# Hybrid diffusion backbone, layer 2: the norm of tile 3 in front of the last scan unit's sums, and the table of further items behind the first item's rows

## The reference, cut to what matters

```python
y = y_f + flip(y_b) + xh * p['ssd_d'][:, None]
return rmsnorm(y * jax.nn.silu(z), p['ssd_norm_w'])            # SSD heads
...
h = head_layernorm(h_f + flip(h_b), p['ml_norm_w'])            # mLSTM heads
out = jax.nn.sigmoid(o) * h
...
xl = xl + mod_l[2] * (yl @ w_out[i])
xl = xl + mod_l[5] * hier_moe(modulated_norm(xl, norm2_w[i], mod_l[3], mod_l[4]), p)
```

## Time and profile before

| | |
|---|---|
| median of 3 runs | 1429.89 us (1426.48 to 1433.22) |
| profiled execution | 1429.08 us |
| its span, first to last instruction | 1427.2 us |
| TensorE matmuls busy | 1200.9 us (84%) |
| VectorE busy | 636.2 us (45%) |
| ScalarE busy | 301.0 us (21%) |
| mean granted clock of TensorE | 0.913 of full speed |

### The profile page before, as it was taken

One profiled execution on the slowest core, in us unless ns is written; L12 is line 12 of the kernel. 1 busy time (PEld: TensorE's weight loads), 2 busy tenths in 40 slices (PEclk: granted clock), 3 DMA queues, 4 the chain that ended last, 5 costly groups with the idle time before them and its releaser, 6 DMA issues. The chain is left out here.

```text
span 1427.2 us, 19787 instructions
## 1 busy us (share of the span) xinstructions
PE 1200.9 (84%) x7656; PEld 789.3 (55%) x7656; DVE 636.2 (45%) x1253; ACT 301.0 (21%) x614; POOL 128.3 (9%) x144
## 2 busy tenths in 40 slices
PE   3899999999899679898877579998869599788882
PEld 1444547987678554544444266467658355445551
DVE  3424763127873542343322264844383634333333
ACT  3302012254442201131101132122432100000001
POOL 0000000000000012212212100000000112222210
PEclk8899999998989769999999879999989589999996
DMA  8743132145641538999999745343472668999993
GB/s 291 199 130 118 59 104 89 57 144 184 199 149 36 226 117 332 398 358 385 383 375 378 285 163 166 118 132 104 154 235 103 227 246 318 397 381 386 394 386 126
DMA packets 148149, 322.18 MB, mean 226 GB/s; under 512 B 28443, under 2 KB 111448, under 8 KB 123864
## 3 DMA queue, kind: packets, MB, share of 16 engines
q1 hardware_dynamic: 136568, 304.86, 59.0%
q0 software_dynamic: 11392, 15.77, 3.4%
q10 hardware_dynamic: 96, 0.26, 0.0%
HBM read 321.11 MB, written 21.23 MB: 240 GB/s over the span
## 5 line engine op out<-in xcount | busy, mean ns | idle before, releaser
L635 PE MATMUL bank<-hT,ring 128*128 128x512 f32 (+1 forms) x544 | 205.9, 536 | 1.5 <-issue 0.8
L635 PE MATMUL bank<-ring,qkT 128*64 128x256 f32 x976 | 156.4, 410 | 33.3 <-DMA ring<-in_moe_w_up 18.5
L635 PE MATMUL bank<-ring,hT 128*128 128x256 f32 (+1 forms) x928 | 180.2, 349 | 3.9 <-DVE ysum L1718 2.1
L635 PEld LDWEIGHTS bank<-ring,hT 128*128 128x128 f32 x928 | 154.0, 193 | 22.6 <-ACT hT L1347 2.7
L635 PEld LDWEIGHTS bank<-hT,ring 128*128 128x128 f32 x544 | 104.1, 193 | 97.9 <-issue 91.1
L1718 DVE TENSOR_TENSOR xbc<-xbc,bank 64x256 f32<-64x256 f32 x65 | 27.5, 423 | 286.7 <-ACT xbc L1347 247.1
L635 PEld LDWEIGHTS bank<-ring,qkT 128*64 128x64 f32 x976 | 97.3, 148 | 62.1 <-issue 19.2
L1347 ACT ACTIVATE xbc<-bank 64x256 f32<-64x256 f32 x65 | 24.6, 378 | 375.5 <-PE bank L635 375.4
L635 PE MATMUL bank<-hT,qkT 128*64 128x256 f32 x496 | 89.3, 398 | 16.8 <-DMA hT<-in_moe_w_up 11.2
L1279 POOL DMA_INDIRECT pair_rows<-hyT,zotok x65 | 59.9, 922 | 433.3 <-DVE xbc L1724 404.7
L635 PE MATMUL bank<-zotok,qkT 128*64 128x256 f32 x256 | 75.2, 459 | 11.5 <-DMA ring<-in_moe_w_up 9.7
(11 more groups left out here) (327 smaller groups left out, 1672.6 us busy)
## 6 DMA issues: line engine op xcount, KB each, us to landing
ring<-in_w_mod SPq DMA_DIRECT2D x40, 1024.0 KB, 7.8
ring<-in_moe_w_down SPq DMA_DIRECT2D x31, 1024.0 KB, 12.6
ring<-in_moe_w_up SPq DMA_DIRECT2D x31, 1024.0 KB, 10.3
ring<-in_moe_w_gate SPq DMA_DIRECT2D x30, 1024.0 KB, 14.7
ring<-in_w_in SPq DMA_DIRECT2D x22, 1024.0 KB, 5.8
hT<-in_moe_w_gate SPq DMA_DIRECT2D x16, 1024.0 KB, 13.8
hT<-in_moe_w_up SPq DMA_DIRECT2D x15, 1024.0 KB, 9.9
hT<-in_moe_w_down SPq DMA_DIRECT2D x15, 1024.0 KB, 12.8
```

Source lines behind the costliest of these rows:

```text
L635: return nc.tensor.matmul(o, a, b, start=s, stop=e, **k)
```

## The change

There are three edits in layer 2's scan and one in both layers' expert stage.

- VectorE: tile 3's norm (`gated`, `head_squares`, `mix_inverse`, `normed`) moves from behind the sums of unit 7 to the head of that unit's pass.
- ScalarE: a square root of a column that nobody reads is issued ahead of tile 3's sum of squares.
- TensorE: the bank counter is set to 0 ahead of the first `mixed`.
- VectorE, both layers: of the ten instructions of the table of further items the last seven move behind the copy of item 0's rows.

```diff
                 if l:
+                    turn[0] = 0
                     mixed(order[0])
...
                 if l:
+                    fn(small[:, 41:42], small[:, 42:43], ACT.Sqrt)
                     gated_squares(3)
                     mix_root(3)
...
                 for u in range(len(units)):
+                    if l and u == last_unit:
+                        gated(3)
+                        head_squares(3)
+                        mix_inverse(3)
+                        normed(3)
                     if u < last_unit:
                         scores(u + 1, 0)
                     ssd_sums(u)
...
                         normed(0)
-                    if l and u == last_unit:
-                        gated(3)
-                        head_squares(3)
-                        mix_inverse(3)
-                        normed(3)
...
                 tt(each, numbers, over(first_of), ALU.is_ge)
-                tt(also, numbers, over(upto), ALU.is_lt)
-                tt(each, each, also, MUL)
-                tt(each, each, over(items[:, 0:32]), MUL)
-                step(V.tensor_reduce(experts_of, each, AX.X, ADD))
-                copy(more_expert, experts_of)
-                ts(upto[:, 31:32], upto[:, 31:32], -1.0 * EXTRA[l], 0.0, ADD, MAX)
-                copy(more_flag, upto[:, 31:32], ("more table", l))
+
+                def more_table():
+                    tt(also, numbers, over(upto), ALU.is_lt)
+                    tt(each, each, also, MUL)
+                    tt(each, each, over(items[:, 0:32]), MUL)
+                    step(V.tensor_reduce(experts_of, each, AX.X, ADD))
+                    copy(more_expert, experts_of)
+                    ts(upto[:, 31:32], upto[:, 31:32], -1.0 * EXTRA[l], 0.0, ADD, MAX)
+                    copy(more_flag, upto[:, 31:32], ("more table", l))
...
                 rows_columns(0)
+                more_table()
                 for j in range(items_now):
```

## The result

The changed kernel takes 1417.28 us in the median of 7 runs (1415.16 to 1420.85); the kernel before, run beside it, 1427.76 (7 runs, 1419.72 to 1433.22). The ratio is 0.9933, 95% interval 0.9908 to 0.9958: 0.67% or 9.6 us faster (6.0 to 13.1). The profiled execution took 1416.92 us with a span of 1415.1 and a mean granted clock of 0.917 (before: 1429.08, 1427.2 and 0.913).

What follows compares the result with a forecast made beforehand. Experts were taken as bound by the weights' stream, which the path before the first item restarts; 4.79 + 1.27 + 2.49 + 1.62 = 10.17 us off the median 1429.89 gave 1419.7, range 1414.5 to 1425.5.

Steps and rivals of the forecast that it cites:

- a clock that stays up: Rival: TensorE's clock does not fall in the shortened gap behind unit 7; 2.2 us more gain, 1417.5 us; chance 0.10.
- The norm in front: End of layer 2's scan, VectorE: tile 3's norm no longer waits behind unit 7's sums; gain 4.79 us.
- The square root's table: End of layer 2's scan, ScalarE: extra root puts the table load into idle time; gain 1.27 us.
- parts 1 and 2: Norm in front plus square root's table, layer 2's scan: TensorE resumes 6.06 us earlier, its gap about 3.8 us.
- What is late next: After layer 2's scan: tile 2's norm (slack 3.2 us), output weights, and the new order's own wait were checked as candidates.
- The bank counter: Layer 2's projection: the reset was taken as 0, with ends of 0.56 us either way.
- The table behind the rows: Expert stages: item 0's rows are copied earlier, 2.49 us in layer 1, 1.62 in layer 2; cover left about 3 us.
- The clock: Layer 2's projection: clock falls again, returns as long after the first product; 0 us, ends 2.2 more gain, 1.8 less.
- VectorE as the bound: Rival: tile 2's norm comes too late, only the table load counts in the scan; 5.4 us remain, 1424.5; chance 0.07.
- the weights as the end: Rival: the weights set the expert stages' end anyway, the change's third part does nothing; 1423.8 us; chance 0.10.
- stay down through the projection: Slower rival: clock stays low in layer 2's projection, 3.7 us per quarter, all seven give 1445.6 us; chance 0.04.
- part 3: Both expert stages: seven table instructions move behind item 0's rows; gain 2.49 us in layer 1, 1.62 in layer 2.

Runs made afterwards that it cites:

- the late norm: Changed kernel with 12 extra copies on VectorE between unit 7's sums and tile 2's norm; one execution timed, 1416.78 us.
- the first filling: Changed kernel with unread identity products on TensorE in gaps of scan, router's stages and around first item; 1410.06 us, ratio 0.9882; timed again 1407.88 us, 0.9879.
- the rows held back: Changed kernel with 22 extra copies on VectorE in front of the copy of item 0's rows, both layers; 1433.11 us, ratio 1.0039.
- the filled versions: Changed kernel with unread identity products in TensorE's gaps: gap behind unit 7 only 1413.66 us; also router and first item 1410.06; more products 1402.47.

## Why the prediction was right

The forecast was a gain of 10.2 us, to 1419.7; the gain is 9.6 us by the ratio (10.5 between the medians), to 1417.28. Of the 2.4 us between the two times 2.1 lie in the base: the kernel before itself came out at 1427.76 beside the changed one, not at 1429.89. So it is chance that the median fell on the number of a rival, 1417.5 for a clock that stays up; the windows at 0.50 rule that rival out.

- **The norm in front, 4.79 us forecast.** 4.80 measured alone. The sums of unit 7, moved behind it, hold nobody up.
- **The square root's table, 1.27 us.** 1.28 to 1.29 alone. The load went into idle time at 1045.18, 7.7 us ahead of the root. The idle time that covers it is not the 9 us that I wrote, which are those of the old order, but 1049.85 - 1045.16 = 4.7, up to tile 3's sum of squares; it was enough, with 3.17 us left. The gap of about 3.8 us that I forecast for parts 1 and 2 together is 3.80, and from unit 7's end to the first product of the projection is 7.39 us in place of 13.47: 6.08 less, where 6.06 was forecast.
- **What is late next: nothing.** Tile 2's norm was to have 3.2 us of slack. It has 4.25 in the profiled execution, because the three quarters ahead of it run 1.1 us longer there, and 3.1 with the late norm, where they don't.
- **The bank counter, 0.** The run without the reset has the same wait.
- **The table behind the rows, 2.49 and 1.62 us.** 2.53 and 1.66; the step from TensorE's end to VectorE's start is 0.10 and not 0.15. The cover in layer 1 is thinner than the 3 us I gave it, 515.66 - 513.93 = 1.7, since item 0's products ran shorter, partly at the higher clock (0.75 over 511 to 516). SP's first load behind the table goes out right behind those products, not at the table's end. In the rows of SP's queue, changed kernel:

```profile
515.76 0.51 SPq L383 DMA_DIRECT2D ktok<-in_hy_pos_w  x1
...
517.77 0.33 SPq L528 DMA_DIRECT2D xtok<-in_moe_w_down  x1
```

- **The clock, 0 with ends of 2.2 more and 1.8 less.** It fell again, as taken from the 4.1 us gap, and came back 5.7 us after the first product, not 3.6: 1.1 us less. This is a term with a wrong value, inside its ends. It isn't a fixed price: with tile 2's norm held back the same stretch took 12.1 us, as in the kernel before, and of two profiled executions of one kernel, that with the first filling, layer 1's item 0 took 5.37 us in one and 3.61 in the other. By the Trainium skill ("TensorE: Matmul & The Clock Gate", Part 1) the chip's window runs freely, so the moment of change differs between runs. These rows agree. At a second place the forecast put the clock at nothing without a word: item 0 itself. Its products took 6.34 and 6.10 us in the two layers before and 4.98 and 5.66 after, the first part of them at the low clock. In layer 2 it took 5.3 to 6.0 us in five profiled executions with the table moved and without filling or delayed rows, and 6.1 to 6.5 in three without the move; in layer 1 the two groups overlap. So part 3 may be worth some half a microsecond a layer more than the wait that it removes.
- **The rivals.** VectorE as the bound falls by the norm alone and by the late norm of tile 2; the weights as the end fall by the rows held back. The clock did not stay down through the projection either. That the clock stays up did not come by itself; it could be bought, with filling.

Not settled: whether the times of the three parts alone add to the time of the whole (4.6 ± 4.4 us against 9.4 ± 3.7). Stage by stage they do, to about 1 us.

## What to carry to other kernels

Where a long stage waits for its first buffers, price an edit in front of it by the wait it takes off the one engine that opens the stage, and check only what is late next; here a sum made from row differences held to a tenth of a microsecond for each wait, but not for the clock behind them. A single execution's span is too coarse for that (here two spans differ by 12.1 us, of which the edits made about 9), so compare stages between two instructions that both kernels have. When the waits are gone as far as they go, look at the clock behind them: unread products in most of the remaining gaps were worth as much again as the whole change, while in one gap alone they moved the fall of the clock into the next.

## What the hardware showed that I had not expected

The scatter between runs of one kernel goes with the granted clock: over 57 timed runs of the kernel before, the mean clock lies between 0.905 and 0.925, correlates with the time at -0.75, and 0.01 of it goes with 4.6 us. Which of the two causes the other, these runs don't separate; the filled versions raise the clock and lower the time together.

VectorE's copies of 128x512 within SBUF took 0.46 us each (10.18 us for 22), where the copy of the same shape out of a PSUM bank takes 0.69.
